# A pass's norm and output scatter, moved behind the next pass's products, in a hybrid layer with 32 experts

## The chip, the cores and the metric

One Trainium2 chip, one core, everything in float32. The metric is the device time of one execution in microseconds. Three runs of the kernel before gave 1115.43, 1116.33 and 1117.3 us; their median is 1116.33 us.

## What is computed

A layer for 512 tokens of width 1024: an input projection, three branches (an RWKV-7 recurrence, a gated spatial unit, a convolution), a gated merge with an output projection, a layer norm, and a mixture of 32 experts with a second layer norm. The change touches the mixture and its norm alone:

```python
x = layer_norm(ALPHA * x + merged @ w_out, ln1_g, ln1_b)
# router: two experts of one group for each token, gates normed to 1
h = silu(xblk @ w_gate[e]) * (xblk @ w_up[e])      # 1024 -> 512
y[token] += gate * (h @ w_down[e])                 # 512 -> 1024
x = layer_norm(ALPHA * x + y, ln2_g, ln2_b)
```

## The kernel before, in words

**Passes.** The mixture runs in passes of up to 64 token slots of one expert. An expert with more than 64 tokens takes a further pass with the same weights. For these inputs there are 33 passes, 0 to 32. The 64 slots lie as 128 partitions of half rows (512 elements): partition s has a token's first half, partition 64 + s its second. A pass needs 6 MB of weights in six 1 MB chunks: four for gate and up, two for down. Four sets of six chunks are in SBUF; SyncE reloads a chunk of set b as soon as TensorE has used it (`reload`, L461, semaphore `s_used`), so loads run up to four experts ahead.

**A pass on each engine.** TensorE (`one_pass` in the tensor block) multiplies the turned tokens `xeT` with gate and up (L1520, 16 matmuls of 64x512, each of which is two records in the trace), turns the next pass's tokens (`turn`, L1501), turns `h_e` (L1529) and multiplies with down (L1540, 8 matmuls, 16 records) into bank 1. VectorE multiplies the two halves of h (L1144, `products`), copies the next `xeT` (`turned`, L1180) and `hT` (L1147) out of PSUM. ScalarE applies Silu (L745), keeps ALPHA times the next tokens in PSUM (`keep_rows`, L740) and copies the gated result to `y_e` (L754).

**A token's two results.** A token has two experts. The pass of the lower one scatters its result to DRAM (`y_rows`, `scatter_lower`, L553); the pass of the upper one gathers it back as `y_low` (`lower_rows`, L544), adds ALPHA x (L1158, "base") and its own `y_e` (L1161, "sum"), norms, and scatters to `out` (`scatter_out`, L564). Every pass does all of it for all slots; indices out of range drop what isn't wanted. The tokens themselves come by a gather (L528). The four transfers of a pass, two gathers and two scatters, are issued by GpSimd, in one order written by hand:

```python
next_tokens(p + 1)     # L525, L528: gather of the tokens of pass p + 2
scatter_lower(p)       # L549, L553
scatter_out(p, first)  # L560, L564: waits for x2 of pass p
lower_rows(p + 1)      # L539, L544: waits until scatter_lower(p) has landed
```

**The norm.** The two halves of a token lie on two partitions, so its statistics are joined by a small product: VectorE makes the statistics of each half row (L1163, L1166, semaphore `s_stat`), TensorE sums the pair (`pair_stats`, L1507, two matmuls of two columns, into `pair`), VectorE makes the deviation's input (L1168 to L1171), ScalarE its root (L757, after a switch to the Sqrt table, L755), and VectorE finishes `x2` (L1172, L1174, L1176). `pair_stats(p)` stands among the gate and up matmuls of pass p, at k = 4 of 8, and joins the statistics of pass p - 1; a last one stands behind all passes. `x2`, `y_e`, `y_low`, `xe` and `hT` have one buffer each: VectorE's base of a pass waits until the scatter from `x2` of the pass before has landed (`s_ost`), ScalarE's copy to `y_e` until the scatter from it has landed (`s_yst`). The tokens kept for the norm have two places in PSUM, but one in a further pass: there `keep_rows` waits for the base of its own pass.

Of the kernel before, what the change touches and what calls it, by code (L numbers as in the profile page):

```python
# [155 lines left out]
def program(nc, x_tok, xT, w_in, par, table, lora, rows, sgu_b, sgu_wT, w_o, w_out, router_w, zeros, w_gu, w_down, out):  # L156
    with ExitStack() as ctx:
# [310 lines left out]
        def _(pool):  # L468
# [98 lines left out]
            def one_pass(p, first=False):  # L567
                next_tokens(p + 1)
                scatter_lower(p)
                scatter_out(p, first)  # L570
                pool.wait_ge(s_ylow, p * 16 + 16)
                lower_rows(p + 1)

# [21 lines left out]
        def _(act):  # L595
# [142 lines left out]
            def keep_rows(p, n):  # L738
                act.wait_ge(s_xe, p * 16 + 16)
                act.activation(x_now[n], xe, ACT.Copy, scale=ALPHA).then_inc(s_xnow, 1)  # L740

            def one_pass(p, n, first=False):
                act.activation(warm[:, 1:2], warm[:, 0:1], ACT.Silu)  # L743
                act.wait_ge(s_hp, p + 1)
                act.activation(h_e, bank[:, 0, 0:FE // 2], ACT.Silu).then_inc(s_silu, 1)  # L745
                act.wait_ge(s_base, p + (2 if n is None else 1))
                keep_rows(p + 1, 0 if n is None else 1 - n)
                if first:
                    act.wait_ge(s_gains, 1)
                else:  # L750
                    act.wait_ge(s_yst, p * 16)
                    act.wait_ge(s_sum, p)
                act.wait_ge(s_yp, p + 2)
                act.activation(y_e, bank[:, 1, :], ACT.Copy, scale=gate_tab[:, bass.ds(p, 1)]).then_inc(s_ye, 1)  # L754
                act.activation(warm[:, 2:3], warm[:, 0:1], ACT.Sqrt)  # L755
                act.wait_ge(s_dev, p + 1)
                act.activation(half_rs[:, 2:3], pair[:, 1:2], ACT.Sqrt, bias=half_rs[:, 1:2], scale=0.5).then_inc(s_root, 1)  # L757

# [9 lines left out]
            with act.If(more > 0):  # L768
                with act.Fori(0, more) as i:
                    one_pass(i + N_EXP, None)  # L770

        @block.vector
        def _(dve):
# [378 lines left out]
            def finish(p, n, first=False):  # L1152
# [12 lines left out]
                dve.memset(half_rs[:, 3:4], 0.0)  # L1165
                dve.bn_aggr(half_mv, ln_stat[:, 0, 0:6]).then_inc(s_stat, 1)  # L1166
                dve.wait_ge(s_pair, p + 2)
                dve.tensor_scalar(mean, pair[:, 0:1], 0.5, None, MUL)  # L1168
# [21 lines left out]
            finish(0, 0, first=True)  # L1190
            products(1)
            finish(1, 1)
            with dve.Fori(1, N_EXP // 2) as i:
                for n in range(2):
                    p = dve.snap(i * 2 + n, min_val=2, max_val=N_EXP - 1)
                    products(p)
                    finish(p, n)
            more = dve.value_load(more_i[0:1, 0:1], min_val=0, max_val=MORE)
            with dve.If(more > 0):
                with dve.Fori(0, more) as i:  # L1200
                    products(i + N_EXP)
                    finish(i + N_EXP, 0)

        @block.tensor
        def _(pe):
# [298 lines left out]
            def pair_stats(p):  # L1504
                pe.wait_ge(s_stat, p + 1)
                for h in range(2):
                    ins = pe.matmul(pair[SLOTS * h:SLOTS * h + SLOTS, :], C("ident_twice"), ln_mv[:, 0, :], start=True, stop=True)  # L1507
                ins.then_inc(s_pair, 1)

            def one_pass(p, b, loads, last):  # L1510
# [3 lines left out]
                for k in range(KT):  # L1514
                    if k == 4:
                        pair_stats(p)
                    if k % 2 == 0:
# [6 lines left out]
                    elif k % 2 == 1 and last:  # L1524
                        ins.then_inc(s_used, 1)
                turn(p + 1)
                pe.wait_ge(s_h, p + 1)
                for c in range(2):
# [91 lines left out]
```

## Time and profile before

| what | value |
|---|---|
| median of three runs | 1116.33 us |
| the profiled execution's own time | 1114.33 us |
| its span in the trace | 1112.6 us |
| instructions | 16547 |
| TensorE busy | 989.5 us (89%) |
| VectorE busy | 472.8 us (42%) |
| ScalarE busy | 283.9 us (26%) |
| GpSimd busy | 208.9 us (19%) |
| DMA | 256.68 MB, mean 231 GB/s |

The span is the time from the first to the last event of the trace; the profiled execution took 1.7 us more than it. Times in the trace count from the span's start. The passes lie between 628 us and the end. Busy shares are means over stages with different limits, so the passes are read on their own.

### The profile page before, as it was taken

The page shows a single profiled execution, that of the slowest core. Times are in us where ns is not written, and L with a number is a line of the kernel's source. Part 1 is how long each engine was busy: PE and PEld are TensorE (multiplying, and loading weights), DVE is VectorE, ACT ScalarE, POOL GpSimd, SP SyncE. Part 2 cuts the span into 40 slices and gives each one's busy share as a digit, 9 for nine tenths or more (in the row PEclk, how much of TensorE's full clock was granted, in tenths as well). Part 3 has the DMA queues.
Part 4 walks back from the last instruction along what each step waited for, and adds up shares of the span by engine and source line. Part 5 has one row for each costly group of instructions (what it writes and reads, how often), then busy time and mean ns, then how long its engine had stood idle before and what let it go on. Part 6 is the DMA issues. An engine that isn't in the chain of part 4 may idle for free.

```text
span 1112.6 us, 16547 instructions
## 1 busy us (share of the span) xinstructions
PE 989.5 (89%) x6068; PEld 456.1 (41%) x6069; DVE 472.8 (42%) x1006; ACT 283.9 (26%) x464; POOL 208.9 (19%) x331
## 2 busy tenths in 40 slices
PE   7999999999999999999993588888888888888785
PEld 3644465466457447444453222322222222222221
DVE  0695542563463363422436143433333333333333
ACT  1123322312322232200001133333333333333232
POOL 3000010010010010033000123333333333333332
PEclk9999999999999999999995699999999999999998
DMA  9332211210320220473709599899999999999992
GB/s 285 109 85 66 60 37 39 76 39 21 75 58 22 57 57 2 159 285 147 303 33 402 186 418 415 334 412 416 416 416 416 415 415 417 415 416 416 417 388 81
DMA packets 93855, 256.68 MB, mean 231 GB/s; under 512 B 15444, under 2 KB 60500, under 8 KB 68976
## 3 DMA queue, kind: packets, MB, share of 16 engines
q1 hardware_dynamic: 81904, 240.54, 56.2%
q0 software_dynamic: 11104, 13.29, 3.5%
q10 hardware_dynamic: 800, 2.15, 0.5%
q8 instruction: 37, 0.61, 0.2%
q14 instruction: 10, 0.08, 0.0%
HBM read 260.90 MB, written 21.23 MB: 254 GB/s over the span
## 4 chain that ended last, share of the span: by engine, by line
PE 51%; DMA 18%; DVE 16%; issue 8%; POOL 3%; ACT 1%; POOLq 1%; SPq 0%; DVEq 0%; ACTq 0%
DMA const<-y_rows,raw 18%; PE proj L1267 11%; PE proj L1226 11%; PE proj L1447 5%; PE bank L1357 5%; PE bank L1435 5%; POOL out L564 3%; DVE raw L1176 2%; PE bank L1520 2%; DVE raw L1161 2%; DVE raw L1158 2%; PE proj L1234 1%; PE proj L1245 1%; DVE arena L897 1%; DVE raw L1172 1%
## 5 line engine op out<-in xcount | busy, mean ns | idle before, releaser
L1267 PE MATMUL proj<-xT_sb,ring 128*128 128x512 f32 x384 | 182.1, 607 | 0.0
L1520 PE MATMUL bank<-arena 128*64 128x512 f32 x544 | 123.7, 596 | 11.0 <-PE bank L1540 11.0
L1226 PE MATMUL proj<-xT_sb,ring 128*128 128x512 f32 (+1 forms) x272 | 119.1, 594 | 0.0
L1158 DVE TENSOR_TENSOR raw<-bank,const 128x512 f32<-128x512 f32 x33 | 22.8, 692 | 196.6 <-DMA const<-y_rows,raw 196.5
L1267 PEld LDWEIGHTS proj<-xT_sb,ring 128*128 128x128 f32 x384 | 68.3, 189 | 68.3 <-issue 64.8
L1226 PEld LDWEIGHTS proj<-xT_sb,ring 128*128 128x128 f32 (+1 forms) x272 | 50.7, 188 | 64.6 <-issue 64.5
L1520 PEld LDWEIGHTS bank<-arena 128*64 128x64 f32 x544 | 39.7, 137 | 80.5 <-issue 80.5
L564 POOL DMA_INDIRECT out<-raw x33 | 33.3, 1008 | 178.3 <-DVE raw L1176 165.1
L1520 PE MATMUL bank<-gates,arena 128*64 128x512 f32 x256 | 59.9, 611 | 6.7 <-PE bank L1540 4.9
L754 ACT ACTIVATE const<-bank,raw 128x512 f32<-128x512 f32 x33 | 22.7, 687 | 154.8 <-PE bank L1540 154.7
L1357 PEld LDWEIGHTS bank<-arena 64*64 64x64 f32 x1536 | 52.8, 134 | 18.2 <-ACT arena L702 9.1
L1357 PE MATMUL bank<-arena 64*64 64x64 f32 (+1 forms) x1536 | 56.5, 228 | 0.0
L1540 PE MATMUL bank<-arena,pass_sb 128*64 128x512 f32 x208 | 48.4, 600 | 8.8 <-DVE pass_sb L1147 7.8
L1435 PE MATMUL bank<-branches,arena 128*128 128x512 f32 x128 | 55.4, 593 | 0.9 <-DVE branches L991 0.9
L499 POOL MEMSET arena<- 64x64 f32 x8 | 1.2, 146 | 291.7 <-DVE arena L914 257.9
L1447 PE MATMUL proj<-arena 128*128 128x512 f32 x128 | 55.4, 592 | 0.0
L553 POOL DMA_INDIRECT y_rows<-const,raw x32 | 33.0, 1032 | 78.7 <-ACT const L754 75.3
L1144 DVE TENSOR_TENSOR pass_sb<-pass_sb,bank 128x256 f32<-128x256 f32 x33 | 13.9, 421 | 74.0 <-ACT pass_sb L745 68.1
L702 ACT ACTIVATE arena<-bank 128x256 f32<-128x256 f32 (+1 forms) x64 | 27.5, 437 | 64.6 <-PE bank L1357 59.6
L743 ACT ACT_TABLE_LOAD x33 | 42.3, 1283 | 1.5 <-issue 0.9
L755 ACT ACT_TABLE_LOAD x33 | 42.3, 1283 | 0.6
L528 POOL DMA_INDIRECT pass_sb<-x_rows,raw x34 | 35.7, 1050 | 28.3 <-POOL raw L525 27.2
(277 smaller groups left out, 1310.8 us busy)
## 6 DMA issues: line engine op xcount, KB each, us to landing
arena<-w_gu SPq DMA_DIRECT2D x64, 1024.0 KB
gates<-w_gu SPq DMA_DIRECT2D x32, 1024.0 KB
arena<-w_down SPq DMA_DIRECT2D x24, 1024.0 KB
ring<-w_in SPq DMA_DIRECT2D x42, 512.0 KB, 3.9
gates<-w_down SPq DMA_DIRECT2D x16, 1024.0 KB
branches<-w_down SPq DMA_DIRECT2D x16, 1024.0 KB
xT_sb<-w_gu SPq DMA_DIRECT2D x16, 1024.0 KB
ring<-w_gu SPq DMA_DIRECT2D x16, 1024.0 KB
```

The costliest lines, as they stand in the source:

```text
L528: pool.indirect_dma_start(xe, None, x1_dram, bass.IndirectOffsetOnAxis(ap=idx_now[:, 0:1], axis=0), bounds_check=last_half_row, oob_is_err ...
L564: pool.indirect_dma_start(out_dram, bass.IndirectOffsetOnAxis(ap=out_now[:, 0:1], axis=0), x2, None, bounds_check=last_half_row, oob_is_er ...
L743: act.activation(warm[:, 1:2], warm[:, 0:1], ACT.Silu)
L755: act.activation(warm[:, 2:3], warm[:, 0:1], ACT.Sqrt)
L1158: dve.tensor_tensor(x2, x_now[n], y_low, ADD).then_inc(s_base, 1)
L1226: ins = pe.matmul(proj[0:w, b, :], ring[:, slot, k, 0:w], xT_sb[:, k, :], start=(k == 0), stop=(k == KT - 1))
L1267: ins = pe.matmul(proj[:, gate_at["bank"], :], ring[:, gate_at["slot"], k, :], xT_sb[:, k, :], start=(k == 0), stop=(k == KT - 1))
L1357: ins = pe.matmul(bank[t, 3 * g + b, j * n:j * n + n], lhsT[t, j, :], rhs[t, j, :], start=True, stop=True)
L1435: ins = pe.matmul(bank[:, 3 * (m % 2) + n, :], wo_sb[:, k0 + k, m * P:(m + 1) * P], src[:, k, :], start=(k == 0), stop=(k == nk - 1))
L1447: ins = pe.matmul(proj[:, n % 2, :], merged[:, k, c * P:(c + 1) * P], wout_sb[:, k, T * i:T * i + T], start=(k == 0), stop=(k == KT - 1))
L1520: ins = pe.matmul(bank[SLOTS * h:SLOTS * h + SLOTS, 0, :], xeT[:, k % 4, SLOTS * (k // 4):SLOTS * (k // 4) + SLOTS], gu[k // 2][:, k % 2, ...
L1540: ins = pe.matmul(bank[SLOTS * h:SLOTS * h + SLOTS, 1, :], hT[:, f % 2, SLOTS * (f // 2):SLOTS * (f // 2) + SLOTS], wd[f // 2][:, f % 2, h ...
```

## The change

The statistics of pass p - 1 are joined behind the gate and up products of pass p and behind the turned tokens of pass p + 1. VectorE's part of the norm becomes a function of its own, `normed`, called for pass p - 1 after the copies of pass p (`products(p)`) and before its base and sum (`finish(p)`). ScalarE's root becomes `deviation` and stands in pass p for p - 1: before the copy to `y_e`, or, in a further pass, before `keep_rows`. GpSimd issues the gather of `y_low` for pass p + 1 before the scatter to `out` of pass p, and that gather now waits for the base of pass p as well, since it overwrites `y_low`. A last `normed` and a last `deviation` stand behind all passes. No instruction of computing is added.

```diff
--- before.py
+++ after.py
@@ -567,9 +567,10 @@
             def one_pass(p, first=False):
                 next_tokens(p + 1)
                 scatter_lower(p)
+                pool.wait_ge(s_ylow, p * 16 + 16)
+                pool.wait_ge(s_base, p + 2)
+                lower_rows(p + 1)
                 scatter_out(p, first)
-                pool.wait_ge(s_ylow, p * 16 + 16)
-                lower_rows(p + 1)
 
             gather(0)
             pool.wait_ge(s_more, 1)
@@ -739,10 +740,18 @@
                 act.wait_ge(s_xe, p * 16 + 16)
                 act.activation(x_now[n], xe, ACT.Copy, scale=ALPHA).then_inc(s_xnow, 1)
 
+            def deviation(p, early=False):
+                if not early:
+                    act.activation(warm[:, 2:3], warm[:, 0:1], ACT.Sqrt)
+                act.wait_ge(s_dev, p + 1)
+                act.activation(half_rs[:, 2:3], pair[:, 1:2], ACT.Sqrt, bias=half_rs[:, 1:2], scale=0.5).then_inc(s_root, 1)
+
             def one_pass(p, n, first=False):
                 act.activation(warm[:, 1:2], warm[:, 0:1], ACT.Silu)
                 act.wait_ge(s_hp, p + 1)
                 act.activation(h_e, bank[:, 0, 0:FE // 2], ACT.Silu).then_inc(s_silu, 1)
+                if n is None:
+                    deviation(p - 1, early=True)
                 act.wait_ge(s_base, p + (2 if n is None else 1))
                 keep_rows(p + 1, 0 if n is None else 1 - n)
                 if first:
@@ -750,11 +759,10 @@
                 else:
                     act.wait_ge(s_yst, p * 16)
                     act.wait_ge(s_sum, p)
+                if not first and n is not None:
+                    deviation(p - 1)
                 act.wait_ge(s_yp, p + 2)
                 act.activation(y_e, bank[:, 1, :], ACT.Copy, scale=gate_tab[:, bass.ds(p, 1)]).then_inc(s_ye, 1)
-                act.activation(warm[:, 2:3], warm[:, 0:1], ACT.Sqrt)
-                act.wait_ge(s_dev, p + 1)
-                act.activation(half_rs[:, 2:3], pair[:, 1:2], ACT.Sqrt, bias=half_rs[:, 1:2], scale=0.5).then_inc(s_root, 1)
 
             act.wait_ge(s_more, 1)
             act.sem_inc(s_ye, 1)
@@ -768,6 +776,7 @@
             with act.If(more > 0):
                 with act.Fori(0, more) as i:
                     one_pass(i + N_EXP, None)
+            deviation(more + (N_EXP - 1))
 
         @block.vector
         def _(dve):
@@ -1164,6 +1173,8 @@
                 dve.wait_ge(s_norm2, p * 4 + 1)
                 dve.memset(half_rs[:, 3:4], 0.0)
                 dve.bn_aggr(half_mv, ln_stat[:, 0, 0:6]).then_inc(s_stat, 1)
+
+            def normed(p):
                 dve.wait_ge(s_pair, p + 2)
                 dve.tensor_scalar(mean, pair[:, 0:1], 0.5, None, MUL)
                 dve.scalar_tensor_tensor(dev_in, pair[:, 0:1], -0.5, half_mv[:, 0:1], MUL, ADD).then_inc(s_norm2, 1)
@@ -1189,17 +1200,21 @@
             dve.wait_ge(s_gains, 1)
             finish(0, 0, first=True)
             products(1)
+            normed(0)
             finish(1, 1)
             with dve.Fori(1, N_EXP // 2) as i:
                 for n in range(2):
                     p = dve.snap(i * 2 + n, min_val=2, max_val=N_EXP - 1)
                     products(p)
+                    normed(p - 1)
                     finish(p, n)
             more = dve.value_load(more_i[0:1, 0:1], min_val=0, max_val=MORE)
             with dve.If(more > 0):
                 with dve.Fori(0, more) as i:
                     products(i + N_EXP)
+                    normed(i + (N_EXP - 1))
                     finish(i + N_EXP, 0)
+            normed(more + (N_EXP - 1))
 
         @block.tensor
         def _(pe):
@@ -1512,8 +1527,6 @@
                 pe.wait_ge(s_xeT, p + 1)
                 gu = [v.rearrange("p (k h n) -> p k h n", k=2, h=2) for v in w_chunk[b][0:4]]
                 for k in range(KT):
-                    if k == 4:
-                        pair_stats(p)
                     if k % 2 == 0:
                         pe.wait_ge(s_w[b][k // 2], loads)
                     for h in range(2):
@@ -1524,6 +1537,7 @@
                     elif k % 2 == 1 and last:
                         ins.then_inc(s_used, 1)
                 turn(p + 1)
+                pair_stats(p)
                 pe.wait_ge(s_h, p + 1)
                 for c in range(2):
                     ins = pe.transpose(bank[:, 3, c * P:(c + 1) * P], h_e[:, c * P:(c + 1) * P], C("ident"))
```

TensorE, one pass (L1520 of before is L1533 of the change, L1501 is L1516, L1507 is L1522, L1529 is L1543, L1540 is L1554). Before:

```order
L1507 MATMUL bank<-arena,const 64x2 [waits half_stats]
L1507 MATMUL bank<-arena,const 64x2
L1520 MATMUL bank<-gates,arena 64x512 [waits w_in0_2]
L1520 MATMUL bank<-gates,arena 64x512 x3
L1520 MATMUL bank<-gates,arena 64x512 [waits w_in0_3]
L1520 MATMUL bank<-gates,arena 64x512 x3
L1498 ISA
L1501 MATMUL bank<-const,pass_sb 128x128 [waits xeT_out,tokens_in]
L1501 MATMUL bank<-const,pass_sb 128x128 x3
L1529 MATMUL bank<-const,pass_sb 128x128 [waits h_ready]
L1529 MATMUL bank<-const,pass_sb 128x128
```

And now:

```order
L1533 MATMUL bank<-gates,arena 64x512 [waits w_in0_2]
L1533 MATMUL bank<-gates,arena 64x512 x3
L1533 MATMUL bank<-gates,arena 64x512 [waits w_in0_3]
L1533 MATMUL bank<-gates,arena 64x512 x3
L1513 ISA
L1516 MATMUL bank<-const,pass_sb 128x128 [waits xeT_out,tokens_in]
L1516 MATMUL bank<-const,pass_sb 128x128 x3
L1522 MATMUL bank<-arena,const 64x2 [waits half_stats]
L1522 MATMUL bank<-arena,const 64x2
L1543 MATMUL bank<-const,pass_sb 128x128 [waits h_ready]
L1543 MATMUL bank<-const,pass_sb 128x128
```

The wait for the statistics has left the gate and up products, and stands between the turned tokens and the wait for h.

GpSimd, the first pass (it stands ahead of the loop and has the loop's order), the difference (line numbers of the four transfers are the same in both):

```order
 L549 COPY raw<-raw 128x1
 L553 DMA y_rows<-const,raw 1024x512
+L539 COPY raw<-raw 128x1
+L544 DMA const<-y_rows,raw 128x512
 L560 COPY raw<-raw 128x1
 L564 DMA out<-raw 1024x512
-L539 COPY raw<-raw 128x1
-L544 DMA const<-y_rows,raw 128x512
```

The gather of `y_low` no longer stands behind the scatter to `out`; the scatter now stands right ahead of the next pass's token gather (L528) and `scatter_lower` (L553).

## Rows read from the trace of the kernel before

**Rows 1.** The page: busy time, then DMA share and GB/s in 40 slices of 27.8 us.

```profile
PE 989.5 (89%) x6068; PEld 456.1 (41%) x6069; DVE 472.8 (42%) x1006; ACT 283.9 (26%) x464; POOL 208.9 (19%) x331
...
DMA  9332211210320220473709599899999999999992
GB/s 285 109 85 66 60 37 39 76 39 21 75 58 22 57 57 2 159 285 147 303 33 402 186 418 415 334 412 416 416 416 416 415 415 417 415 416 416 417 388 81
```

**Rows 2.** The page: the chain that ended last, by line.

```profile
DMA const<-y_rows,raw 18%; PE proj L1267 11%; PE proj L1226 11%; PE proj L1447 5%; PE bank L1357 5%; PE bank L1435 5%; POOL out L564 3%; DVE raw L1176 2%; PE bank L1520 2%; DVE raw L1161 2%; DVE raw L1158 2%; PE proj L1234 1%; PE proj L1245 1%; DVE arena L897 1%; DVE raw L1172 1%
```

**Rows 3.** Timeline, one pass: start us, us, engine, line, op, tiles [idle before <-releaser].

```profile
876.70 0.16 DVE L1168 TENSOR_SCALAR half_rs<-bank 128x1 f32<-128x1 f32 x1 [0.39 <-PE bank L1507]
...
879.52 1.01 POOL L564 DMA_INDIRECT out<-raw  x1 [5.23 <-DVE raw L1176]
...
880.07 0.66 PE L1501 MATMUL bank<-const,pass_sb 128*128 128x128 f32 x4
...
881.57 1.07 POOL L544 DMA_INDIRECT const<-y_rows,raw  x1 [0.84 <-POOL raw L539]
881.63 0.42 DVE L1147 COPY pass_sb<-bank 128x256 f32<-128x256 f32 x1
...
882.11 3.65 PE L1540 MATMUL bank<-gates,pass_sb 128*64 128x512 f32 x16 [0.52 <-issue]
...
883.66 1.05 POOL L528 DMA_INDIRECT pass_sb<-x_rows,raw  x1 [0.82 <-POOL raw L525]
...
887.40 1.03 POOL L553 DMA_INDIRECT y_rows<-const,raw  x1 [2.49 <-ACT const L754]
...
887.95 0.69 DVE L1158 TENSOR_TENSOR raw<-bank,const 128x512 f32<-128x512 f32 x1 [5.89 <-DMA const<-y_rows,raw]
...
890.37 0.28 PE L1507 MATMUL bank<-arena,const 128*64 128x2 f32 x4 [0.28 <-DVE arena L1166]
```

**Rows 4.** DMA queues from 891.25 to 893.75: packets, MB, share of 16 engines.

```profile
q0 software_dynamic: 80, 0.21, 21.1%
```

**Rows 5.** Timeline of PE: first matmuls of passes 0, 1, 2 and 32.

```profile
628.30 5.30 PE L1520 MATMUL bank<-gates,arena 128*64 128x512 f32 x16 [1.77 <-DVE arena L1180]
...
643.53 3.65 PE L1520 MATMUL bank<-arena 128*64 128x512 f32 x16 [0.75 <-PE bank L1540]
...
657.02 3.65 PE L1520 MATMUL bank<-arena 128*64 128x512 f32 x16 [0.69 <-PE bank L1540]
...
1088.10 3.65 PE L1520 MATMUL bank<-ring,arena 128*64 128x512 f32 x16 [0.68 <-PE bank L1540]
```

**Rows 6.** Timeline of SyncE's queue: the loads after the doubled expert.

```profile
717.51 2.04 SPq L461 DMA_DIRECT2D arena<-w_gu  x2
```

**Rows 7.** Windows (length, busy of PE, PEld, DVE, ACT, POOL; last: PEclk, DMA share, GB/s).

```profile
714.00:716.00 2.00, 2.00 (x12) 0.71 (x10) 0.00 (x0) 0.25 (x1) 0.75 (x2) 1.00 0.40 142
716.00:718.00 2.00, 2.00 (x12) 0.59 (x10) 1.45 (x2) 1.92 (x3) 0.76 (x1) 1.00 0.01 4
718.00:720.00 2.00, 2.00 (x15) 0.60 (x12) 1.54 (x7) 0.19 (x1) 0.47 (x2) 1.00 0.74 152
1094.00:1095.00 1.00, 1.00 (x6) 0.29 (x4) 0.64 (x1) 0.72 (x1) 0.00 (x0) 1.00 0.10 41
1095.00:1096.00 1.00, 1.00 (x6) 0.14 (x2) 0.00 (x0) 0.77 (x2) 0.52 (x1) 1.00 0.00 0
```

**Rows 8.** Timeline of the last pass, 32.

```profile
1092.46 3.63 PE L1520 MATMUL bank<-xT_sb,arena 128*64 128x512 f32 x16
...
1097.54 1.07 POOL L544 DMA_INDIRECT const<-y_rows,raw  x1 [0.85 <-POOL raw L539]
...
1098.06 3.65 PE L1540 MATMUL bank<-branches,pass_sb 128*64 128x512 f32 x16 [0.52 <-DVE pass_sb L1147]
...
1100.40 0.69 DVE L1158 TENSOR_TENSOR raw<-bank,const 128x512 f32<-128x512 f32 x1 [2.39 <-DMA const<-y_rows,raw]
...
1102.72 0.69 DVE L1161 TENSOR_TENSOR raw<-raw,const 128x512 f32<-128x512 f32 x1 [1.63 <-ACT const L754]
```

## The prediction

> **What bounds the kernel now.** I read the page first. From about 640 us on the DMA engines are full, at some 416 GB/s in nearly every slice [rows 1], so the stage of the passes has a bound that no engine order can lift. Then the chain of waits: its largest line is not a matmul but the gather of `y_low`, 18% of the span [rows 2]. In the timeline of one pass one sees why: the joined statistics are followed by the norm and the scatter to `out` (VectorE 876.70, GpSimd 879.52), then the gather of `y_low` (881.57), whose data let VectorE start the base at 887.95; the statistics are ready 2.42 us later, and TensorE, inside its gate and up products, waited for them until 890.37 [rows 3]. This is a closed ring: 876.70 to 890.37 is 13.67 us, and the joined result is read 0.3 us later, so 14.0 us in this pass. Over the passes it gives 1088.10 - 643.53 = 444.57 us for 31 passes, 14.34 us each. Pass 1, for which no wait is seen, took 657.02 - 643.53 = 13.49 us [rows 5]. So two things are close together: TensorE's ring at 14.34 us, and the weights.
>
> How close, the end shows. A set of weights is 6.29 MB, for which the DMA engines need 15.1 us (6.29 MB at 416 GB/s [rows 1]), and an estimated 16 with the tokens of a pass (twice the 0.21 MB of [rows 4]); that is more than a pass. The passes live on a lead of four sets and eat it up. In the last pass the queue's load ends at 1094 to 1095 us: the DMA share is 0.10 in that microsecond and 0.00 in the next [rows 7]. The engine that ends last serves the six chunks in turn; 1 MB over 16 engines at 416 GB/s is 2.5 us a chunk, so the last gate and up chunk has landed about 5 us before, near 1090. TensorE came to it halfway through 1092.46 to 1096.09, at 1094.3 [rows 8]. The slack is some 4 us (4.3 less 0.3 for the wake-up).
>
> **The change, part by part.**
>
> *The ring is cut.* The wait for statistics leaves the gate and up products, and the `y_low` gather no longer follows the scatter to `out`. TensorE's own work then gives 13.4 us a pass: 13.49 as above, less about 0.1 of the two small matmuls, which now stand in the time in which TensorE waits for h anyway (from the end of the turned tokens, 880.73, to the turned h at about 881.15).
>
> *New rings.* The norm of pass p - 1 now starts when the copy of hT of pass p is done (881.63 + 0.42 = 882.05), and `x2`, GpSimd's order and the token buffer close rings through it. Durations [rows 3]: norm to issue of the scatter 879.52 - 876.70 = 2.82 us; spacing of two issues on GpSimd 881.57 - 879.52 = 2.05 us; issue to arrival 887.95 - 881.57 = 6.4 us for a gather. The scatter from `y_e` issued at 887.40 has its last packets before 893.75, also 6.35 us [rows 4], so I take 6.4 us for each of the four transfers. Turned tokens to end of the hT copy is 882.05 - 880.07 = 1.98 us. From that:
> - Through `x2`: scatter 6.4, base to statistics 2.4, then the product of h, its turning and copy (1.3, from 880.7 to 882.05), norm 2.8: 12.9 us.
> - Through the tokens: 2.05 behind the scatter to `out` the next token gather is issued, 6.4 to arrive, 2.0 to the end of the hT copy, 2.8: 13.3 us.
> - Through GpSimd: scatter to `out`, token gather, scatter from `y_e` (2 x 2.05), its arrival 6.4 (GpSimd must see it before it gathers `y_low`), 0.7 more for GpSimd to start an issue, gather and index copy 2.05: 13.3 us.
> - Through ScalarE: the root now waits for the scatter from `y_e` of the pass before: 4.1 + 6.4, 0.2 for the table's warm-up, 2.3 from the root to the issue: 13.0 us.
>
> All four lie under or at TensorE's 13.4. With jitter among five nearly equal rings I take **13.6 us** a pass, against 14.34. The bounds: 13.4 (TensorE alone) and, if the transfers, issued closer together, take 1 us more each, 14.4.
>
> *What that buys.* 31 passes x 0.74 = 23 us, if nothing else bound. The weights do. TensorE may come forward by the slack of 4 us, and by what the loads come forward. These were never idle after 640 us but once: the expert with two passes frees no chunk for a pass, SyncE's next load went out at 717.51 [rows 6], and the DMA share was 0.40, 0.01, 0.74 in the windows of 714 to 720 [rows 7]. The engine that is last was thus idle for some 3 us, from 716 to 719. Pass 6 follows five gaps between passes; at 0.6 us or more each the load is issued 3 us earlier and the idle time is gone. So the last chunk lands 3 us earlier, and the end of the last down product moves by -(4 + 3) = **-7 us**. The 16 us left of the 23 are waits for weights in the last four or five passes. The bounds are 0 (the passes don't get shorter) and -23 (no bound by weights).
>
> *What it costs at the end.* In the last pass nothing covers the moved norm. Before, its base started at 1100.40 and its sum at 1102.72 [rows 8]. Now, with the hT copy ending at about 1098.0: norm 2.8 to the scatter's issue, then its arrival. With idle DMA engines a gather took 1100.40 - 1097.54 = 2.86 us, and I take this for the scatter. That puts the base at 1103.7, 3.3 us later, and since this is a further pass, whose `keep_rows` and copy to `y_e` wait for the base, the sum is later by the same **+3.3 us**. The chain behind it is unchanged. The bounds: +2 (half the arrival hidden) and +6.8 (a loaded arrival of 6.4). The Trainium skill, in "DMA: Bandwidth & Descriptors", section "Anatomy of one DMA — SWDGE (gpsimd) path", gives a transfer issued by GpSimd about 2.0 us fixed and the rest by its size; by it this term would be an estimated 0.6 us smaller. The row's 2.86 us is the longer one, and it is used.
>
> The edits of VectorE's and ScalarE's order cost nothing besides: both are idle over half of the time, and each does the same operations. No DMA is added.
>
> **The sum.** -7 + 3.3 = -3.7 us. On the profiled execution: 1112.6 of span to 1108.9, and 1114.33 to 1110.6 of its own time. The median of the runs is 2.0 us above the profiled execution, and the sum is put on it: 1116.3 - 3.7 = **1112.6 us**. About 0.2%, 2.2 us, is what a measurement of this kernel can tell from no change.
>
> **The rivals.**
>
> *The new rings are as long as the old (slower).* Four transfers are now issued one behind the other at 2.05 us, where the old order had a pause ahead of the scatter from `y_e` (883.66 to 887.40 [rows 3]). If each arrives later for that, the ring through GpSimd decides, since the wait for the scatter from `y_e` stands on it. The point from which the whole change loses is a pass of 14.24 us: 31 x 0.1 = 3.1 us is all that pays the tail. At 14.4 the passes cost +2, the tail +3.3: 1121.5 us. For it: the margin is under 1 us on an arrival that I have as a single value. Against it: the four transfers use under a tenth of the engines' time. Chance 0.20.
>
> *The loads don't come forward.* If the idle time of 3 us stays, or the last chunks land less than 4 us ahead of their use, the gain is about -4 + 3.3 = -0.7: 1115.6 us, no difference. The slack is worked out from one engine's order, not seen. Chance 0.13.
>
> *The clock falls in the waits for weights.* The granted clock is 1.00 in every window of [rows 7], with TensorE busy throughout. In the last passes it will wait some 2.5 us in each (16 less 13.6, and more where a chunk is late). At the half clock of pass 0 half of the gate and up matmuls took 5.30 us, against 3.65 [rows 5]; such a loss behind the last chunk, on the rest of gate and up and on down, is +2.5 us: 1115.1 us, no difference. The Trainium skill's "TensorE: Matmul & The Clock Gate", section "HAM oscillation — how this bites in real kernels", tells of just this, a clock that falls in each wait for a weight slice. No row here shows a wait of that length at full load, so it stays open. Chance 0.04.
>
> *The weights bind less than I think.* If the fast engines' chunks are what matters, or the lead is larger, more of the 23 us shows: -10 or so, 1106 us. Against it: the loads end at 1095 whatever TensorE does. Chance 0.05.
>
> **How the numbers follow.** My forecast has 0.58. With the rival of a larger gain, faster by over 0.2% has 0.63; the two small ones give 0.17 for within 0.2%; slower has 0.20. The range goes from 1108.5 (the slack 3 us larger, with a cheaper tail) to 1119 (into the slower case, at passes of 14.3 us), and leaves out the ends of the first and last rival.
>
> **What would show it.** Right: TensorE's passes 13.4 to 13.8 us apart up to about pass 27, no wait for statistics in gate and up, the DMA share near 1 from 712 to 720, then waits of TensorE for weights in the last passes, passes 16 us apart there, the last down product beginning near 1091, and base to sum in the last pass starting 5.7 us behind the hT copy. Wrong: passes over 14.2 us apart; a GpSimd that waits for the scatter from `y_e`; a DMA dip that stays; an end of the loads that does not move.

## The result, and the profile after

The change is faster: 1109.93 us (five runs, 1108.53 to 1111.02) against 1115.43 us for the kernel before on the same chip (five runs, 1114.21 to 1117.3), a ratio of 0.9948 with an interval of 0.9933 to 0.9963. That is 5.5 us. The profiled execution took 1111.02 us, with a span of 1109.3 us, 3.3 us less than before.

The page of the change: busy times, the slices of DMA share and GB/s, and the chain that ended last, by engine and by line.

```profile
PE 993.4 (90%) x6068; PEld 464.9 (42%) x6069; DVE 469.6 (42%) x1006; ACT 279.3 (25%) x461; POOL 219.2 (20%) x331
...
DMA  9332211210220220473709599999999999999992
GB/s 274 121 78 73 58 40 40 71 44 21 76 55 24 57 58 2 154 271 136 320 35 399 167 400 415 397 411 416 417 416 415 415 416 416 415 415 415 419 397 87
...
PE 52%; DMA 14%; SPq 12%; DVE 8%; issue 8%; POOL 4%; ACT 1%; POOLq 1%; DVEq 0%; ACTq 0%
PE proj L1282 11%; SPq L461 11%; PE proj L1241 11%; DMA y_rows<-const,raw 8%; PE proj L1462 5%; PE bank L1372 5%; PE bank L1450 5%; PE bank L1533 3%; DMA xT_sb<-w_gu 3%; DMA out<-raw 2%; PE bank L1554 1%; PE proj L1249 1%; POOL pass_sb L528 1%; POOL const L544 1%; PE proj L1260 1%
```

Against [rows 1] two things stand out. The slice that held 334 GB/s (from 695 to 723 us) now holds 397: the dip behind the doubled expert is nearly gone. And the chain [rows 2] no longer runs through the gather of `y_low`: in its place stand the scatter from `y_e` (8%), and behind that SyncE's queue of weight loads (12%). The rest is as it was; the stage of the passes ends with the loads.

One pass of the change in the timeline (start us, us, engine, line, operation, idle before and its releaser), to be laid beside [rows 3]:

```profile
863.95 1.02 POOL L564 DMA_INDIRECT out<-raw  x1 [0.92 <-DVE raw L1187]
...
865.95 1.05 POOL L528 DMA_INDIRECT pass_sb<-x_rows,raw  x1 [0.79 <-POOL raw L525]
...
868.04 1.02 POOL L553 DMA_INDIRECT y_rows<-const,raw  x1 [0.85 <-POOL raw L549]
...
870.54 0.69 DVE L1167 TENSOR_TENSOR raw<-bank,const 128x512 f32<-128x512 f32 x1 [7.43 <-DMA out<-raw]
...
872.61 0.65 PE L1516 MATMUL bank<-const,pass_sb 128*128 128x128 f32 x4
...
873.20 0.28 PE L1522 MATMUL bank<-arena,const 128*64 128x2 f32 x4
...
873.68 0.44 PE L1543 MATMUL bank<-const,pass_sb 128*128 128x128 f32 x2 [0.21 <-DVE pass_sb L1153]
874.16 0.42 DVE L1156 COPY pass_sb<-bank 128x256 f32<-128x256 f32 x1
...
875.27 1.05 POOL L544 DMA_INDIRECT const<-y_rows,raw  x1 [3.27 <-DMA y_rows<-const,raw]
875.53 0.16 DVE L1185 RECIPROCAL half_rs<-half_rs 128x1 f32<-128x1 f32 x1
...
877.39 1.01 POOL L564 DMA_INDIRECT out<-raw  x1 [0.87 <-POOL raw L560]
```

The statistics are now joined (L1522) between the turned tokens and the turned h, and TensorE hardly waits there: 0.65 us of turning, 0.28 us of joining, then h, 0.21 us later. VectorE's norm runs from 874.50 to 876.48. GpSimd's order is scatter to `out` (863.95), tokens (865.95), scatter from `y_e` (868.04), then a wait of 3.27 us for that scatter's arrival, the gather (875.27), and the next scatter to `out` (877.39): 13.44 us round.

The starts of the turned tokens give the passes: from 652.35 to 994.66 us, 25 passes at 13.69 us each (before, over the same passes, 650.66 to 1007.68, 14.28 us). Two of these 25, behind the doubled expert, took 14.85 and 15.16 us. The first of them ended with a wait of 1.49 us for the gathered tokens, and behind it the granted clock fell (0.60 and 0.55 in the windows from 737 to 741 us), so that the down product of the second took 5.35 us instead of 3.65. Then come 14.5, 16.5, 15.8, 16.5, 16.0 and 15.9 us. In those TensorE waits for weights, as this piece of the pass from 1041.51 to 1058.01 shows, with a wait ahead of each chunk of gate and up:

```profile
1047.87 1.94 PE L1533 MATMUL bank<-arena 128*64 128x512 f32 x8 [0.68 <-DMA arena<-w_gu]
1050.17 1.94 PE L1533 MATMUL bank<-arena 128*64 128x512 f32 x8 [0.36 <-DMA arena<-w_gu]
1052.88 1.94 PE L1533 MATMUL bank<-arena 128*64 128x512 f32 x8 [0.78 <-DMA arena<-w_gu]
1056.14 1.94 PE L1533 MATMUL bank<-arena 128*64 128x512 f32 x8 [1.32 <-DMA arena<-w_gu]
1058.01 0.66 PE L1516 MATMUL bank<-const,pass_sb 128*128 128x128 f32 x4
```

Each row is one chunk (8 records, 1.94 us); the waits in brackets end with `DMA arena<-w_gu`. The first of the four, 0.68 us, is no longer than the one that stands there in every pass; the other three are new. The granted clock held all the same, as the windows' row over the last passes shows (behind the busy times: PEclk, DMA share, GB/s):

```profile
1039.00:1089.00 50.00, 38.88 (x180) 12.09 (x182) 16.71 (x45) 14.06 (x24) 15.79 (x24) 1.00 0.92 379
```

The windows of the old dip, to be compared with [rows 7]:

```profile
714.00:716.00 2.00, 2.00 (x12) 0.68 (x10) 0.00 (x0) 0.74 (x2) 1.15 (x3) 1.00 0.82 287
716.00:718.00 2.00, 2.00 (x12) 0.72 (x10) 0.00 (x0) 0.00 (x0) 0.87 (x1) 1.00 0.95 377
718.00:720.00 2.00, 1.28 (x6) 0.14 (x2) 1.78 (x3) 0.38 (x1) 0.53 (x1) 1.00 0.95 332
```

The end of the last pass, to be compared with [rows 8]:

```profile
1089.91 0.66 PE L1516 MATMUL bank<-const,pass_sb 128*128 128x128 f32 x4
...
1091.95 3.65 PE L1554 MATMUL bank<-branches,pass_sb 128*64 128x512 f32 x16 [0.52 <-DVE pass_sb L1156]
...
1094.62 1.01 POOL L564 DMA_INDIRECT out<-raw  x1 [3.18 <-DVE raw L1187]
1097.40 0.69 DVE L1167 TENSOR_TENSOR raw<-bank,const 128x512 f32<-128x512 f32 x1 [3.62 <-DMA out<-raw]
...
1098.21 0.60 ACT L741 ACTIVATE bank<-pass_sb 128x512 f32<-128x512 f32 x1 [5.64 <-DVE raw L1167]
1098.74 0.67 ACT L765 ACTIVATE const<-bank,raw 128x512 f32<-128x512 f32 x1
...
1099.51 0.69 DVE L1170 TENSOR_TENSOR raw<-raw,const 128x512 f32<-128x512 f32 x1 [1.42 <-ACT const L765]
```

From the turned tokens of the last pass to its sum it is 9.60 us; before it was 1102.72 - 1096.03 = 6.69. The base (1097.40) is released by the scatter to `out`, and kept tokens and `y_e` follow behind it one by one.

**Where the time went.** From the second turned tokens (of pass 0) to the last, the profile of before has 1096.03 - 637.09 = 458.9 us, the change 1089.91 - 638.95 = 451.0: -8.0 us. From there to the end 16.6 us became 19.4: +2.8 us. That is -5.2 us, close to the 5.5 us of the medians. The span shows only -3.3 because this one execution of the change came to its turned tokens of pass 0 1.9 us later, for nothing that the change touches but the product of two columns: most of it is gate and up of pass 0, 10.1 us against 8.9, run partly at the half clock in both. A second profile of the change (below) has this point at 636.30.

### The profile page after: what moved, and what is told of

It is laid out like the page before. It is cut to its first block, busy times and chain, and to the rows that moved or that the text cites. A ratio compares the mean times of both kernels' runs of the same rounds, so it can differ in the third digit from the quotient of the medians.

```text
span 1109.3 us, 16552 instructions
## 1 busy us (share of the span) xinstructions
PE 993.4 (90%) x6068; PEld 464.9 (42%) x6069; DVE 469.6 (42%) x1006; ACT 279.3 (25%) x461; POOL 219.2 (20%) x331
## 4 chain that ended last, share of the span: by engine, by line
PE 52%; DMA 14%; SPq 12%; DVE 8%; issue 8%; POOL 4%; ACT 1%; POOLq 1%; DVEq 0%; ACTq 0%
PE proj L1282 11%; SPq L461 11%; PE proj L1241 11%; DMA y_rows<-const,raw 8%; PE proj L1462 5%; PE bank L1372 5%; PE bank L1450 5%; PE bank L1533 3%; DMA xT_sb<-w_gu 3%; DMA out<-raw 2%; PE bank L1554 1%; PE proj L1249 1%; POOL pass_sb L528 1%; POOL const L544 1%; PE proj L1260 1%
## 5 line engine op out<-in xcount | busy, mean ns | idle before, releaser
L1533 PE MATMUL bank<-arena 128*64 128x512 f32 x544 | 122.1, 596 | 16.2 <-PE bank L1554 9.5
L1533 PEld LDWEIGHTS bank<-arena 128*64 128x64 f32 x544 | 43.0, 137 | 95.1 <-issue 82.8
L1533 PE MATMUL bank<-gates,arena 128*64 128x512 f32 x256 | 60.2, 622 | 8.4 <-PE bank L1554 4.8
L752 ACT ACTIVATE pass_sb<-bank 128x256 f32<-128x256 f32 x33 | 12.7, 383 | 201.1 <-PE bank L1533 201.1
L1554 PE MATMUL bank<-arena,pass_sb 128*64 128x512 f32 x208 | 50.0, 618 | 8.8 <-DVE pass_sb L1156 8.8
L544 POOL DMA_INDIRECT const<-y_rows,raw x33 | 34.6, 1049 | 114.2 <-DMA y_rows<-const,raw 107.0
L528 POOL DMA_INDIRECT pass_sb<-x_rows,raw x34 | 35.8, 1053 | 27.4 <-POOL raw L525 26.3
L606 ACT ACTIVATE gates<-proj 128x512 f32<-128x512 f32 x24 | 14.3, 596 | 104.7 <-PE proj L1282 104.7
```

The source lines that it names most:

```text
L528: pool.indirect_dma_start(xe, None, x1_dram, bass.IndirectOffsetOnAxis(ap=idx_now[:, 0:1], axis=0), bounds_check=last_half_row, oob_is_err ...
L544: pool.indirect_dma_start(y_low, None, y_dram, bass.IndirectOffsetOnAxis(ap=up_now[:, 0:1], axis=0), bounds_check=last_half_row, oob_is_er ...
L1533: ins = pe.matmul(bank[SLOTS * h:SLOTS * h + SLOTS, 0, :], xeT[:, k % 4, SLOTS * (k // 4):SLOTS * (k // 4) + SLOTS], gu[k // 2][:, k % 2, ...
L1554: ins = pe.matmul(bank[SLOTS * h:SLOTS * h + SLOTS, 1, :], hT[:, f % 2, SLOTS * (f // 2):SLOTS * (f // 2) + SLOTS], wd[f // 2][:, f % 2, h ...
```

## The experiments

The kernels of one table row ran on the same chip as the kernel before. A pass is the distance of the turned tokens, as a mean over the middle passes. Where two values stand, the passes are of two kinds.

| kernel | us | ratio to before (interval) | pass, us |
|---|---|---|---|
| the change | 1109.93 | 0.9948 (0.9933 to 0.9963) | 13.7 |
| e1, product moved alone | 1247.65 | 1.1189 (1.117 to 1.1209) | 18.5 |
| e2, gather's order alone | 1140.53 | 1.0236 (1.0214 to 1.0258) | 15.1 |
| e3, change with old gather order | 1154.58 | 1.0348 (1.0329 to 1.0367) | 15.5 |
| e4, base in place | 1106.23 | 0.9923 (0.9907 to 0.9938) | 13.6 |
| e5, the change again | 1109.01 | 0.9942 (0.9927 to 0.9956) | 13.6 |
| e6, before with short loads | 1106.01 | 0.9915 (0.99 to 0.993) | 14.0 |
| e7, change with short loads | 1094.31 | 0.9807 (0.9789 to 0.9824) | 13.5 |
| e8, e1 with TensorE kept busy | 1202.42 | 1.0773 (1.0755 to 1.0791) | 16.4 and 18.1 |

**e1: the product moved alone.** The kernel before with this edit:

```diff
-                    if k == 4:
-                        pair_stats(p)
...
                 turn(p + 1)
+                pair_stats(p)
                 pe.wait_ge(s_h, p + 1)
```

> The kernel before with one edit: TensorE's joining product stands behind the turned tokens; VectorE, ScalarE and GpSimd keep their order, so the norm of the pass before (2.0 us on VectorE, 2.4 us with the join) now runs ahead of the product of h. Theory of five rings: TensorE's own 13.4 us grow by 2.4 to 15.8 us a pass, 31 passes, +45 us: about 1160 us. Rival (the wait inside gate and up was the whole cost, and where the norm stands does not matter): 13.4 to 13.6 us a pass, the weights bind, about 1107 us.

Measured: 132 us slower, a pass of 18.5 us. The direction of the theory holds and the rival is out, but the size is three times as large. The timeline shows one term that was left out and the windows (the last three numbers: PEclk, DMA share, GB/s) show another, the larger one.

```profile
908.14 0.28 PE L1507 MATMUL bank<-arena,const 128*64 128x2 f32 x4
...
910.66 0.36 ACT L745 ACTIVATE pass_sb<-bank 128x256 f32<-128x256 f32 x1
...
911.13 0.42 DVE L1144 TENSOR_TENSOR pass_sb<-pass_sb,bank 128x256 f32<-128x256 f32 x1 [0.67 <-ACT pass_sb L745]
...
911.61 0.69 PE L1528 MATMUL bank<-const,pass_sb 128*128 128x128 f32 x2 [3.18 <-DVE pass_sb L1144]
...
912.81 3.68 PE L1539 MATMUL bank<-arena,pass_sb 128*64 128x512 f32 x8 [0.52 <-DVE pass_sb L1147]
```

```profile
907.00:909.00 2.00, 1.43 (x12) 0.62 (x8) 0.49 (x4) 0.02 (x1) 0.00 (x0) 1.00 1.01 418
911.00:913.00 2.00, 0.88 (x4) 0.48 (x6) 1.45 (x3) 0.52 (x2) 1.20 (x2) 0.63 1.01 426
913.00:915.00 2.00, 2.00 (x6) 0.58 (x6) 0.00 (x0) 0.00 (x0) 1.26 (x2) 0.50 0.90 313
919.00:921.00 2.00, 1.28 (x8) 0.57 (x8) 1.53 (x3) 1.64 (x2) 0.16 (x1) 1.00 0.97 387
```

The root of the norm now comes on ScalarE just ahead of Silu, so the Silu table (1.28 us) is loaded inside the path, and TensorE waits 3.18 us for h, where it waited 0.42 before: 2.8 us more, against the 2.4 costed. And with that wait the granted clock fell: 1.00 at 907 to 909, 0.63 and 0.50 from the end of the wait on, back at 1.00 by 919. It did so in each of the 32 passes that have this wait. The down product, 3.65 us in the change, took 6.39 us here (the row above and a second one of 2.92 us, which overlap), and 4.8 to 6.4 us in the others, 5.7 in the mean. Without a fall of the clock such a pass takes 16.35 us (this is seen in e8, next); the 2.0 us of the down product bring it to 18.4, of the 18.5 measured. Single passes differ (17.7 to 19.4 us), as they spend more or less time at the lower clock.

**e8: the same, with TensorE kept busy in the wait.** This edit on top of e1 (the added wait is for ScalarE's copy out of bank 1, which the turns overwrite):

```diff
                 pair_stats(p)
+                pe.wait_ge(s_ye, p + 1)
+                for c in range(16):
+                    pe.transpose(bank[:, 1, (c % 4) * P:(c % 4 + 1) * P], C("ident"), C("ident"))
                 pe.wait_ge(s_h, p + 1)
```

> The kernel of the first experiment (joining product moved alone), and 16 turns of the identity by TensorE (128 columns each, into PSUM bank 1, whose content is overwritten by the next down product) behind the joining product, in the 3.2 us in which TensorE stood still there. Theory: the granted clock, 0.50 to 0.66 in four windows after that wait, stays at 1.00; the down product takes 3.65 us again instead of 6.6, and a pass 15.8 to 16.4 us instead of 18.4: some 2 to 2.6 us x 30 less, 1170 to 1187 us. Rival (the slow matmuls behind the wait come from late weights or a port, not from the clock): no change, 1247 us or more.

Measured: 45 us less than e1, short of the 60 to 77 expected. The passes are of two kinds, near 16.4 us (17 of 32) and near 18.05 us (12). The turns filled 2.0 of the 3.2 us; what was left of the wait is in the second row:

```profile
994.49 1.97 PE L1528 MATMUL bank<-const 128*128 128x128 f32 x16
...
997.74 0.44 PE L1531 MATMUL bank<-const,pass_sb 128*128 128x128 f32 x2 [1.28 <-DVE pass_sb L1144]
```

After this wait of 1.28 us the clock held in 19 of 31 passes, with the down product at 3.65 us (16.35 us for most of these passes), and fell in 12, with 5.35 us and 18.05 us a pass. The rival (weights or a port) is out: the same matmuls under the same loads ran at full speed in every pass in which the clock held. Why it holds in one pass and not in the next stays open. The theory had it hold in all; the 12 falls, at 1.7 us each, are 20 us, and the time missed the slow end of the expectation, 1187 us, by 15.

**e2: the gather's order alone.** The kernel before, with GpSimd's `one_pass` as in the change (`lower_rows(p + 1)`, with its waits, ahead of `scatter_out`).

> The kernel before with one edit: GpSimd gathers y_low of the next pass ahead of the scatter to out. Theory: GpSimd then sits in the wait for the scatter from y_e (7.2 us from issue to next issue), the scatter to out goes out late, and the base waits for it: 14.7 us a pass against 14.34, +11 us, about 1127 us. Rival (the gather of y_low behind the scatter was the ring, cutting it alone is enough): 13.5 us a pass, about 1107 us.

Measured: 25 us slower, where 11 was expected; the rival is out. Two passes in the timeline:

```profile
930.48 1.02 POOL L553 DMA_INDIRECT y_rows<-const,raw  x1 [3.29 <-ACT const L755]
...
937.69 1.05 POOL L544 DMA_INDIRECT const<-y_rows,raw  x1 [5.64 <-DMA y_rows<-const,raw]
...
939.81 1.01 POOL L564 DMA_INDIRECT out<-raw  x1 [0.88 <-POOL raw L560]
...
946.77 0.69 DVE L1159 TENSOR_TENSOR raw<-bank,const 128x512 f32<-128x512 f32 x1 [8.09 <-DMA out<-raw]
```

The wait for the scatter from `y_e` (930.48 to 937.69, 7.21 us, as costed) holds back the scatter to `out` until 939.81, and the base waits for that until 946.77. The ring closes over two passes, a short one and a long one. In the long one TensorE waits some 2 us for the statistics in the middle of gate and up, and what follows depends on the clock. Here is the second half of gate and up in two long passes:

```profile
919.59 3.63 PE L1521 MATMUL bank<-arena 128*64 128x512 f32 x16
...
949.43 5.10 PE L1521 MATMUL bank<-gates,arena 128*64 128x512 f32 x16
```

In the first the granted clock was 1.00 throughout; in the second it fell at 949, with the end of a wait of 2.48 us, and was 0.50 in the window from 950 to 952. From 848 us on, the long passes without a fall take 15.5 to 15.9 us, which with the 13.5 to 13.9 us of the short ones makes 14.7 in the mean, just the expected value. The long passes with a fall take 17.4 to 17.9 us, some 1.9 more; there are seven of them, 13 us in all. An eighth fall stands in a pass of 21.0 us, of which more below. So the ring was priced right, and nearly all of the 14 us beyond the expected 11 is the clock.

**e3: the change with the old gather order.** The change, with `scatter_out(p)` ahead of `lower_rows(p + 1)` again.

> The change with GpSimd's order put back (scatter to out, then gather of y_low). Theory: the token gather is issued 4.1 us behind the scatter to out instead of 2.05, so the ring through the tokens is 4.1 + 6.4 + 2.0 + 2.8 = 15.3 us a pass, and with the tail's +3 us the whole is +33: about 1148 us. Rival (GpSimd's order is of no weight once the product has moved): as the change, about 1110 us.

Measured: 39 us slower than before, where 33 was expected; passes of 15.3 to 15.7 us in the middle, against the 15.3 worked out for the ring through the tokens. The clock fell here too, in 16 passes, each time with a wait of TensorE for the tokens (1.2 to 3.9 us); the down product then took 4.9 to 6.3 us, and the next wait for tokens was shorter by most of that. The rival is out: with the norm moved, GpSimd's order is worth 45 us, such falls included. So each half of the change alone (the order in e2, the moved norm in e3) is a loss, and the gain is in the two together.

**e4: the base in place.** Aimed at the tail:

```diff
-                if not first:
-                    dve.wait_ge(s_ost, p * 16)
-                dve.tensor_tensor(x2, x_now[n], y_low, ADD).then_inc(s_base, 1)
+                dve.tensor_tensor(y_low, x_now[n], y_low, ADD).then_inc(s_base, 1)
                 dve.wait_ge(s_base, p + 2)
                 dve.wait_ge(s_ye, p + 2)
-                dve.tensor_tensor(x2, x2, y_e, ADD).then_inc(s_sum, 1)
+                if not first:
+                    dve.wait_ge(s_ost, p * 16)
+                dve.tensor_tensor(x2, y_low, y_e, ADD).then_inc(s_sum, 1)
...
-                pool.wait_ge(s_base, p + 2)
+                pool.wait_ge(s_sum, p + 1)
                 lower_rows(p + 1)
```

> The change, but the base is written into y_low's own place, and only the sum writes x2: the base no longer waits for the scatter to out, the sum does; the gather into y_low waits for the sum instead of the base. Theory: the tail's 2.9 us come from base, kept tokens and copy to y_e being lined up behind the scatter's arrival; now only the sum is, 2.1 us earlier: about 1107.8 us, passes unchanged at 13.6 and bound by the weights at the end. Rival (the tail is set by the norm's later start alone): no change against the change, 1109.9 us.

```profile
1087.22 0.66 PE L1516 MATMUL bank<-const,pass_sb 128*128 128x128 f32 x4
...
1091.01 0.68 DVE L1165 TENSOR_TENSOR const<-bank,const 128x512 f32<-128x512 f32 x1
...
1093.13 0.69 ACT L765 ACTIVATE const<-bank,raw 128x512 f32<-128x512 f32 x1 [0.72 <-PE bank L1554]
...
1094.73 0.69 DVE L1170 TENSOR_TENSOR raw<-const 128x512 f32<-128x512 f32 x1 [3.04 <-DMA out<-raw]
```

The base (L1165) now starts 3.79 us behind the last turned tokens, `y_e` is ready while the scatter is under way, and only the sum waits for it: 1094.73 - 1087.22 = 7.51 us against 9.60, 2.1 us less, as expected. The passes are as before (13.6 us). At 1106.23 us it is faster than the kernel before by 0.8%. Against the change the profiles give 2.0 us (spans of 1104.5 and, for e5, 1106.5), with the stretch up to the last turned tokens the same within 0.1 us, so the rival (the norm's later start alone) is out for the tail. The two ran on different occasions; the ratio between them is not measured directly, and their intervals against before overlap.

**e5, e6 and e7: are the weights the bound at the end?** In e6 and e7 each reload leaves out the last eighth of a chunk, so these kernels compute the mixture partly with the weights of four experts earlier. The one edit, to before and to the change:

```diff
-                    sp.dma_start(w_chunk[b][c], src.rearrange("a p n -> (a p) n")).then_inc(s_w[b][c], 16)
+                    sp.dma_start(w_chunk[b][c][:, 0:CHUNK * 7 // 8], src.rearrange("a p n -> (a p) n")[:, 0:CHUNK * 7 // 8]).then_inc(s_w[b][c], 16)
```

> The change itself again, beside the next two. Both theories: about 0.995 of the kernel before.

> The kernel before, where each reload brings only the first 7/8 of a chunk (the last eighth keeps the weights of four experts earlier, so the mixture is computed with partly wrong weights; all matmuls are there). A set then needs about 14.2 us of the DMA engines instead of 16. Theory: the weights did not bind here, the ring did: passes 14.2 to 14.34 us, 0 to -4 us against the kernel before. Rival (the DMA engines set the pass already before): -10 us or more.

> The change with the same 7/8 reloads (same part of the mixture left out). Theory: the last six passes, 95.3 us between their turned tokens where 6 x 13.6 = 81.6 would do, no longer wait for weights: 13.7 us less than the change, about 1096 us, 13.6 us a pass to the end. Rival (the rest of the gain was lost in the new rings or the tail, not to the weights): about 1109 us.

e7 came to 1094.31 us, 14.7 less than e5 beside it (13.7 expected, 1096). Its last six passes are 13.9, 13.9, 16.3, 14.8, 13.4 and 13.4 us long, and no wait of TensorE ends with a load of weights. The two long ones are not for weights; the section on the prediction comes back to them. The slices show the DMA engines through long before the end (the last weights land at 1047 us):

```profile
GB/s 287 114 78 66 68 40 40 59 59 21 58 58 42 39 74 5 155 274 116 339 46 275 248 329 414 326 355 391 415 414 414 413 414 413 414 412 415 388 82 20
```

So the change's remaining gain was held back by the weights; the rival for e7 is out. e6 was sized wrong: 9.8 us faster than before (an interval of 7.8 to 11.2), where 0 to 4 was expected and the rival had 10 or more. By the number alone the rival is not out, and by the trace its mechanism is: TensorE waited for no weights in e6, nor had it in before. What became shorter is the ring, from 14.23 us a pass (the 20 passes from 737 us on) to 14.04, and to 13.5 in the last three passes, after the loads had ended. The ring of before has a transfer in it, the gather of `y_low`. From its issue to the start of the base it took 6.61 us in the mean of those 20 passes in before (6.37 to 6.93), 6.42 us in e6, and 2.9 us once the loads had ended: 0.19 us less, and the pass is 0.19 us shorter. The theory had held the arrival constant. So the load on the DMA engines did cost the kernel before something, through this arrival. Set against each other, e7 is 11.7 us faster than e6: that is what the change is worth with the shorter loads. The prediction's bound for a case without waits for weights, 23 us less the tail, had about 20; part of the difference is that the ring of before got shorter too.

The dip, in e5's profile, is gone altogether (the second number from the right, the DMA share):

```profile
714.00:716.00 2.00, 2.00 (x12) 0.70 (x10) 0.47 (x1) 0.00 (x0) 0.24 (x1) 1.00 1.01 418
716.00:718.00 2.00, 0.91 (x6) 0.20 (x3) 1.78 (x5) 0.60 (x2) 0.53 (x1) 1.00 0.95 346
718.00:720.00 2.00, 1.48 (x12) 0.91 (x12) 1.79 (x7) 1.82 (x4) 0.00 (x0) 0.90 1.04 430
```

The 0.90 in the last row is the start of the one fall of the granted clock in e5's passes, at 719.6 us, behind a wait of 1.09 us for tokens.

## Why the prediction was right

- **The ring is cut, 13.4 us of TensorE's own.** Right. The first pass of the change (638.95 to 652.35) and the first two of e5 take 13.4 us, before the other rings have closed.
- **New rings, 13.6 us a pass.** Right: 13.7 in the first profile (13.6 from 750 us on), 13.6 in the second. The arrival of 6.4 us, taken from one pass, is on the low side: 6.6 is the mean of 20 passes, in before for the gather and in the change from the scatter to `out` to the base. The ring through GpSimd, worked out at 13.3, reads 13.44 in the pass shown, with the spacing (2.0 to 2.1 us) and the arrival (868.04 to 875.27, 7.2 us with GpSimd's own start) as costed. e2 and e3 show that the same prices, in another order, give the rings worked out for them: 14.7 us where the clock held, and 15.5 in the mean for 15.3.
- **The weights bind at the end, in the last four or five passes.** Right: the first wait for a weight chunk stands at 1007 us, and five passes of 15.8 to 16.5 us follow (six of 15.7 to 16.7 in e5, from 990 us on). e7 shows that with shorter loads 14.7 us more come out.
- **The slack of 4 us and the 3 us of the dip, -7 us.** Measured -8.0 (and 1087.12 - 636.30 = 450.8 in e5, -8.1). The slack was nearly right. The last chunk of gate and up landed at 1090.5 us before and was used at 1094.3, so the slack was 3.8 us less the wake-up. What was a little too small is the 3 us of the dip. Counted from the turned tokens of pass 0, that chunk landed at 1090.5 - 637.1 = 453.4 us before and at 1088.0 - 638.9 = 449.1 us in the change, and in e5 at 1085.2 - 636.3 = 448.9: the loads came forward by 4.4 us rather than 3. With 0.3 us for the wake-up, 3.5 + 4.4 = 7.9 us. Over 640 to 720 us the DMA share rose from 0.96 to 1.00, which is 3.2 us of the 80; where the other 1.2 us came from was not traced.
- **The tail, +3.3 us.** Measured +2.8. The scatter's arrival was 2.78 us (1094.62 to 1097.40) against the 2.86 taken, and the norm to the issue 2.81 against 2.82. The 0.5 us counted too much are small pieces: 7.49 us from the turned tokens to the base (7.7 forecast), 2.11 from base to sum (2.32 taken), 9.8 from the sum to the end (9.9 before). The prediction also made an estimate from the Trainium skill, "DMA: Bandwidth & Descriptors", section "Anatomy of one DMA — SWDGE (gpsimd) path": a term 0.6 us smaller. The scatter moved 0.21 MB, and by the page's figures (2.0 us, and the bytes at 436 GB/s) that is an estimated 2.5 us, which would make the term 0.4 us smaller; the trace has 2.78.
- **The sum, -3.7 us.** Measured -5.5, with an interval of 4.1 to 7.5 us. The two terms erred by 1.0 and 0.5 us, in the same direction. The mechanism was right, the sum at the small end. The absolute time, forecast as 1112.6 and measured as 1109.93, is off by 0.9 us more, because the median of before came out as 1115.43 us over five runs, not 1116.33.
- **The rivals.** New rings as long as the old: no, though e2 and e3 show how near they are, with one transfer more in line. Loads that don't come forward: no. Weights that bind less: no. A falling clock: not where the rival had it. The waits for weights come in pieces between chunks, of up to 1.3 us (1.5 in e5), and the clock stayed at 1.00 there. It fell once in each profile of the change, earlier and behind a wait for tokens (at 737 us behind 1.49 us; in e5 at 720 behind 1.09), and cost the down product 1.7 us. That pass lies far ahead of the ones in which the weights decide, so it did not show in the time. e1 shows that one wait of 3.2 us in each pass makes the clock fall in each. The Trainium skill's section that the prediction names for this rival (in "TensorE: Matmul & The Clock Gate", "HAM oscillation — how this bites in real kernels") tells of a kernel that waits for data longer than it computes, and of a clock that falls in each such wait. The waits for weights here are shorter than the products between them (1.94 us a chunk), and the trace of the change does not show such a fall.
- **One thing the profile had and the prediction did not use:** the pass of before from 1036.26 to 1053.29 took 17.03 us. `x2` was ready at 1034.88, and GpSimd started the scatter to `out` only at 1038.38, 3.5 us later where about 1 is usual, with the releaser "issue". Why is not shown; it is not the end of GpSimd's loop, which has three more passes to go. The same pass is long in e2, e3 and e6 (21.0, 18.1 and 16.8 us). In the change it lies under the waits for weights. The cut ring alone does not take such a delay up, as e7 shows, where no weights are waited for. There the gather of `y_low` was late in the same way (at 1020.71, 6.59 us idle before, releaser "issue"), two passes took 16.3 and 14.8 us, and TensorE waited for the tokens and then ran its down product at the lower clock:

```profile
1031.40 0.66 PE L1516 MATMUL bank<-const,pass_sb 128*128 128x128 f32 x4 [3.06 <-DMA pass_sb<-x_rows,raw]
...
1033.17 5.35 PE L1554 MATMUL bank<-gates,pass_sb 128*64 128x512 f32 x16 [0.53 <-DVE pass_sb L1156]
```

## What to carry to other kernels

List every closed ring that a moved step will stand on, the transfers and the queue's issue spacing included, and price each from one pass of the timeline; a step that leaves one engine's path may close a longer ring on another, and half of such a change can cost more than the whole gives. Then look for the resource that runs at its limit throughout (here the loads): its slack at the end, not the sum of the savings per pass, is the gain. And cost the last pass on its own, since nothing covers there what was moved behind the next. Where a changed order makes TensorE wait 1 to 3 us in one piece, read the granted clock as well: in e1, e2 and e8 the waits themselves were priced nearly right, and the clock was the larger part of the miss.

## What the runs showed of the hardware

- **The clock after a pause.** A wait of 3.18 us in each pass brought TensorE's granted clock from 1.00 to 0.50 in every pass (e1). 16 small turns in the pause, which left 1.28 us, kept it at 1.00 in 19 of 31 passes (e8). In e2, waits of 1.9 to 2.5 us did it in some passes and not in others, and one of 3.11 us did not. In the change it fell behind single waits of 1.49 and 1.09 us for tokens (in e5 the latter), and never in the waits for weights, of up to 1.5 us and about 2.5 us a pass in sum. So the length of a wait alone doesn't tell. A fall cost 1.7 us where a whole down product, 3.65 us, ran into it (5.35 us).
- **Arrival under load.** From issue to the start of its reader a transfer of half rows took 6.4 to 7.0 us with the DMA engines full, 6.6 in the mean (before and the change), and 2.8 to 2.9 us with them idle, in the tails of before and of the change. With loads shortened by an eighth, still at 411 GB/s, it took 6.42 us, and the pass that hangs on it became 0.19 us shorter (e6).
- **Full DMA engines do not mean that the loads bind.** Before, the DMA share was near 1 from 640 us on, but for the dip at 714 to 720, and TensorE waited for no load; the kernel was living on its lead of four sets, of which 3.8 us were left at the last chunk of gate and up.
